# Where the split operands of the matmuls begin in SBUF: input at 128-byte lines, narrow products' weights 64 bytes on

## What is computed

```python
for i in range(DEPTH):                     # 4 layers
    kind, j = i % N_MIXERS, i // N_MIXERS  # mixers: MLA, MoBA, SSD, MLA
    h = rmsnorm(x, norm_mix[i])
    x = x + mixer(h)                       # MLA: 16 heads; MoBA: 8 heads; SSD: Mamba-2 scan, inner width 2048
    x = x + sq_relu_mlp(rmsnorm(x, norm_mlp[i]), mlp_w1[i], mlp_w2[i])
return rmsnorm(x, norm_final)

def sq_relu_mlp(h, w1, w2):
    a = jax.nn.relu(h @ w1)                # 1024 -> 4096
    return (a * a) @ w2                    # 4096 -> 1024
```

## Time and profile before

| | us |
|---|---|
| median of 3 runs | 1313.64 |
| lowest, highest | 1311.1, 1315.05 |
| span of the profiled execution | 1312.0 |
| TensorE matmul busy in it | 1286.5 (98%) |
| DVE busy | 891.4 (68%) |
| ACT busy | 671.6 (51%) |

### The profile page before, as it was taken

The page is one execution under the profiler, slowest core; times in us unless marked ns, Lnnn a source line. Parts: engine busy times, 40 slices in busy tenths (PEclk is TensorE's granted clock), DMA queues, the critical chain, the costliest instruction groups (busy, mean ns, idle before and its releaser), DMA issues.

```text
span 1312.0 us, 18369 instructions
## 1 busy us (share of the span) xinstructions
PE 1286.5 (98%) x7578; PEld 1126.3 (86%) x7578; DVE 891.4 (68%) x1180; ACT 671.6 (51%) x861; POOL 43.5 (3%) x58
## 2 busy tenths in 40 slices
PE   6999999999999999999999999999999999999998
PEld 5888888888999888887999888888887888888886
DVE  5877666665666666666899886766667876666664
ACT  5555554444555454444776644544445645454442
POOL 3000000000000000000101110000000000000000
PEclk9999999999999999999999999999999999999999
DMA  9744465555845475545574643755554334565540
GB/s 289 143 168 148 141 232 201 193 192 161 233 149 180 132 254 192 192 165 160 181 222 141 203 149 119 249 191 192 191 180 140 117 130 130 168 231 193 192 161 32
DMA packets 146067, 230.93 MB, mean 176 GB/s; under 512 B 7683, under 2 KB 112429, under 8 KB 145984
## 3 DMA queue, kind: packets, MB, share of 16 engines
q1 hardware_dynamic: 143136, 221.66, 50.8%
q0 software_dynamic: 2848, 8.10, 2.9%
HBM read 227.08 MB, written 2.65 MB: 175 GB/s over the span
## 4 chain that ended last, share of the span: by engine, by line
PE 88%; DVE 7%; DMA 1%; issue 1%; ACT 1%; POOL 1%; SPq 0%; POOLq 0%; DVEq 0%; ACTq 0%
PE bank L982 15%; PE acc L902 12%; PE acc L903 12%; PE acc L906 12%; PE bank L987 8%; PE bank L590 7%; PE bank L591 7%; PE bank L592 7%; DVE wlo L573 2%; PE bank L1402 1%; PE bank L1105 1%; PE bank L795 1%; PE bank L1408 1%; PE bank L1090 1%; DMA raw<-in_mla_w_in 1%
## 5 line engine op out<-in xcount | busy, mean ns | idle before, releaser
L573 DVE TENSOR_TENSOR wlo<-raw,whi 128x2048 fp32r<-128x2048 f32 (+2 forms) x207 | 464.7, 2255 | 139.6 <-ACT whi L557 139.5
L557 ACT ACTIVATE whi<-raw 128x2048 fp32r<-128x2048 f32 (+2 forms) x207 | 386.8, 1879 | 45.8 <-PE acc L906 44.2
L982 PE MATMUL bank<-hsplit,whi 128*128 128x512 f32 x896 | 212.2, 389 | 0.0
L903 PE MATMUL acc<-wlo,uhi 128*128 128x512 f32 x512 | 200.1, 391 | 0.0
L902 PE MATMUL acc<-whi,uhi 128*128 128x512 f32 x512 | 199.6, 390 | 0.0
L982 PEld LDWEIGHTS bank<-hsplit,whi 128*128 128x128 f32 x896 | 168.2, 188 | 34.9
L906 PE MATMUL acc<-whi,ulo 128*128 128x512 f32 x512 | 159.2, 390 | 0.0
L590 PE MATMUL bank<-hsplit,whi 128*128 128x256 f32 (+2 forms) x540 | 154.5, 286 | 0.3 <-DVE xn L1980 0.3
L592 PE MATMUL bank<-hsplit,wlo 128*128 128x256 f32 (+2 forms) x540 | 151.4, 280 | 0.0
L591 PE MATMUL bank<-hsplit,whi 128*128 128x256 f32 (+2 forms) x540 | 151.4, 280 | 0.0
L1027 ACT ACTIVATE relu<-bank 128x512 f32<-128x512 f32 x56 | 33.5, 598 | 188.9 <-PE bank L987 188.9
(11 more groups left out here) (252 smaller groups left out, 1813.4 us busy)
## 6 DMA issues: line engine op xcount, KB each, us to landing
raw<-in_mlp_w SPq DMA_DIRECT2D x128, 1024.0 KB, 5.5
raw<-in_ssd_w_in SPq DMA_DIRECT2D x18, 1024.0 KB, 5.4
raw<-in_mla_w_o SPq DMA_DIRECT2D x16, 1024.0 KB, 4.9
raw<-in_mla_w_ukv SPq DMA_DIRECT2D x8, 1024.0 KB, 5.8
raw<-in_moba_w_qkv SPq DMA_DIRECT2D x16, 512.0 KB, 5.3
raw<-in_ssd_w_out SPq DMA_DIRECT2D x8, 1024.0 KB, 4.9
raw<-in_mla_w_uq SPq DMA_DIRECT2D x8, 768.0 KB, 6.0
raw<-in_mla_w_in SPq DMA_DIRECT2D x4, 1024.0 KB, 7.5
```

Of the source, the lines that this page charges most:

```text
L557: nc.scalar.activation(whi[:, s, lo:e], raw[:, s, lo:e], ACT.Copy).then_inc(w_hi_done[s], 1)
L573: nc.vector.tensor_tensor(wlo[:, s, lo:e], raw[:, s, lo:e], whi[:, s, lo:e].bitcast(F32), ALU.subtract).then_inc(w_split[s], 1)
L903: nc.tensor.matmul(acc[t][half][:], lh, wl[:, k, n], start=False, stop=False)
L982: nc.tensor.matmul(ps, w[0][:, k, m * P:(m + 1) * P], hflat[:, k].rearrange("p a n -> p (a n)"), start=k == 0, stop=False)
```

## The change

`hsplit` becomes a plain array of 8 rows of 512 elements, used alike by all stages: input always at a line. The slots of `whi` and `wlo` become 32 elements longer (8320 bytes, 65 lines), and each unit's high and low part begin at an offset of 0 or 16 elements (64 bytes) in their slot, by kind: `ca`, `cb`, `down`, `wo`, `so` and `ukv` at 0 in both; `up` at 0 in `whi` and 16 in `wlo`; `kpe` with the first `uq`, the other `uq`, `mv`, `mqk`, `dt`, `cv` and `z` at 16 in both. ACT and DVE write, and `hi_lo` reads, at these offsets. The built program has the same instructions in the same order on all engines; `wlo` moves by 512 bytes, `x`, `xn`, `gbc` and `hsplit` by 1024, all else stays. As 65 is odd, slots 1 and 3 now begin at 0 modulo 256 and slots 0 and 2 at 128.

```diff
-        whi = sb("whi", [P, SLOTS, UNIT], F32R)
-        wlo = sb("wlo", [P, SLOTS, UNIT], F32R)
+        whi = sb("whi", [P, SLOTS, UNIT + 2 * HALF_LINE], F32R)
+        wlo = sb("wlo", [P, SLOTS, UNIT + 2 * HALF_LINE], F32R)
...
-        hrows = sb("hsplit", [P, KD, 2 * SEQ + 32], F32R)
-        hsplit = hrows[:, :, 16:16 + 2 * SEQ].rearrange("p k (a n) -> p k a n", a=2)
-        hflat = hrows[:].rearrange("p k n -> p (k n)")[:, 0:KD * 2 * SEQ].rearrange("p (k a n) -> p k a n", k=KD, a=2)
+        hsplit = sb("hsplit", [P, KD, 2, SEQ], F32R)
...
+        def start_of(kind):
+
+            if kind in ("ca", "cb", "down", "wo", "so", "ukv"):
+                return (0, 0)
+            return (0, HALF_LINE) if kind == "up" else (HALF_LINE, HALF_LINE)
...
         def hi_lo(key):
             off, a, b = view[key]
             s = first[key] % SLOTS
-            return (whi[:, s, off:off + a * b].rearrange("p (a b) -> p a b", a=a),
-                    wlo[:, s, off:off + a * b].rearrange("p (a b) -> p a b", a=a))
+            hi, lo = (off + start for start in starts[first[key]])
+            return (whi[:, s, hi:hi + a * b].rearrange("p (a b) -> p a b", a=a),
+                    wlo[:, s, lo:lo + a * b].rearrange("p (a b) -> p a b", a=a))
...
-                lo = 0
+                lo, high = 0, whi[:, s, starts[n][0]:starts[n][0] + e]
...
-                nc.scalar.activation(whi[:, s, lo:e], raw[:, s, lo:e], ACT.Copy).then_inc(w_hi_done[s], 1)
+                nc.scalar.activation(high[:, lo:e], raw[:, s, lo:e], ACT.Copy).then_inc(w_hi_done[s], 1)
...
-                nc.vector.tensor_tensor(wlo[:, s, lo:e], raw[:, s, lo:e], whi[:, s, lo:e].bitcast(F32),
+                nc.vector.tensor_tensor(low[:, lo:e], raw[:, s, lo:e], high[:, lo:e].bitcast(F32),
                                         ALU.subtract).then_inc(w_split[s], 1)
...
-        def split_input(j):
-
-            h = hflat if deferred(j) else hsplit
-            return h[:, :, 0, :], h[:, :, 1, :]
```

More of the change, by code:

```diff
@@ L34 @@
 UNIT = 2048
+HALF_LINE = 16
 AHEAD = 3
@@ L276, in build @@
         units, first = [], {}
+        starts = []
         view = {}
+        def start_of(kind):
+            if kind in ("ca", "cb", "down", "wo", "so", "ukv"):
+                return (0, 0)
+            return (0, HALF_LINE) if kind == "up" else (HALF_LINE, HALF_LINE)
         def unit(key, a, b, *srcs):
             first[key] = len(units)
+            starts.append(start_of(key if key == "dt" else key[0]))
             view[key] = (0, a, b)
@@ L288, in unit_of_two @@
             off, parts = 0, []
+            starts.append(start_of(keys[0][0]))
             for key, (a, b), src in zip(keys, shapes, srcs):
@@ L552, in act_splits @@
                     act.wait_ge(w_used[s], k)
-                lo = 0
+                lo, high = 0, whi[:, s, starts[n][0]:starts[n][0] + e]
                 if n in in_halves:
                     lo = e // 2
-                    nc.scalar.activation(whi[:, s, :lo], raw[:, s, :lo], ACT.Copy).then_inc(half_hi_done, 1)
-                nc.scalar.activation(whi[:, s, lo:e], raw[:, s, lo:e], ACT.Copy).then_inc(w_hi_done[s], 1)
+                    nc.scalar.activation(high[:, :lo], raw[:, s, :lo], ACT.Copy).then_inc(half_hi_done, 1)
+                nc.scalar.activation(high[:, lo:e], raw[:, s, lo:e], ACT.Copy).then_inc(w_hi_done[s], 1)
                 split_to["act"] += 1
@@ L565, in dve_splits @@
                 e = units[n][0] * units[n][1]
-                lo = 0
+                lo, high, low = 0, whi[:, s, starts[n][0]:starts[n][0] + e], wlo[:, s, starts[n][1]:starts[n][1] + e]
                 if n in in_halves:
@@ L569, in dve_splits @@
                     dve.wait_ge(half_hi_done, n + 1)
-                    nc.vector.tensor_tensor(wlo[:, s, :lo], raw[:, s, :lo], whi[:, s, :lo].bitcast(F32),
+                    nc.vector.tensor_tensor(low[:, :lo], raw[:, s, :lo], high[:, :lo].bitcast(F32),
                                             ALU.subtract).then_inc(half_split, 1)
                 dve.wait_ge(w_hi_done[s], k + 1)
-                nc.vector.tensor_tensor(wlo[:, s, lo:e], raw[:, s, lo:e], whi[:, s, lo:e].bitcast(F32),
+                nc.vector.tensor_tensor(low[:, lo:e], raw[:, s, lo:e], high[:, lo:e].bitcast(F32),
                                         ALU.subtract).then_inc(w_split[s], 1)
@@ L635, in act_scale_upper @@
                                  scale=rstd[:, j * T + t:j * T + t + 1]).then_inc(xn_upper_done, 1)
-        def split_input(j):
-            h = hflat if deferred(j) else hsplit
-            return h[:, :, 0, :], h[:, :, 1, :]
         def act_tr(act, j, t):
-            hhi, _ = split_input(j)
             for half in range(2):
@@ L719, in dve_tr @@
         def dve_tr(dve, j, t, halves=(0, 1)):
-            hhi, hlo = split_input(j)
             for half in halves:
@@ L981, in pe_up @@
                 for k in range(KD):
-                    nc.tensor.matmul(ps, w[0][:, k, m * P:(m + 1) * P], hflat[:, k].rearrange("p a n -> p (a n)"),
+                    nc.tensor.matmul(ps, w[0][:, k, m * P:(m + 1) * P], hsplit[:, k].rearrange("p a n -> p (a n)"),
                                      start=k == 0, stop=False)
@@ L986, in pe_up @@
                 for k in range(KD):
-                    mm = nc.tensor.matmul(ps[:, 0:SEQ], w[1][:, k, m * P:(m + 1) * P], hflat[:, k, 0, :], start=False,
+                    mm = nc.tensor.matmul(ps[:, 0:SEQ], w[1][:, k, m * P:(m + 1) * P], hsplit[:, k, 0, :], start=False,
                                           stop=k == KD - 1)
```

## The result

| | before | after |
|---|---|---|
| median, us | 1314.35 | 1321.75 |
| lowest, highest | 1311.1, 1315.71 | 1321.31, 1322.35 |
| span of the profiled execution | 1312.0 | 1319.7 |

The ratio is 1.0063, its 95% interval 1.0048 to 1.0078: the change makes the kernel 0.63% slower, about 7.4 us for the medians, 7.7 us for the spans. The prediction was 1303.0 us, range 1299.5 to 1310.5, so it missed the sign as well.

The account below looks back on a forecast made before the run. TensorE's summed matmul steps were taken to bound the kernel. The terms summed to -10.8 us, taken as -10.5: from the 1312.0 us span, plus 1.6 us around or between executions, to 1303 us, range 1299.5 to 1310.5.

Parts of the forecast that it names:

- item 10: ACT and DVE accessing most units 64 bytes past a line: 0, hidden under PE in any case.
- Item 9: Last L982 of each round, followed by a load of shifted low weights: 56 wide steps, 0 to +0.3 us, taken +0.15.
- Item 2: Narrow L987 products of the MLPs: 840 steps from 119.4 to 113.8 ns, -4.7 us.
- the first rival: Pair isn't symmetric: shifted stationary weights bring nothing in the mixers, half in items 2 to 4; 1310.5 us, chance 0.08.
- Item 1: Mixers' `mqk`, `cv`, `z`: 1248 narrow steps from 117.0 to 113.8 ns, -4.0 us.
- item 5: `kpe`: 48 steps from 117.0 to 113.8 ns, -0.15 us.
- Item 3: First two `up` units, low weights shifted: 128 of 384 steps from 120.0 to 113.8 ns, -0.8 us.
- Item 4: `uq` by head in MLA: 192 steps from 120.0 to 113.8 ns, -1.2 us; `ukv` 0.
- Item 6: MoBA's values, weights moving from 64 bytes past a line: 192 steps from 113.3 to 117.0 ns, +0.7 us.
- Item 7: Rotary part of `uq`, same pair as MoBA's values but from 120.0 ns: 96 steps, -0.3 us.
- Item 8: Wide `ca` and `cb`, input now at a line: 96 steps, -0.5 us if the input's place is the cause, else 0.
- two rivals: Odd slots slow some 1550 wide products: 5.5 ns each, 1311.5 us, chance 0.07; or 13.4 ns each, 1324 us, chance 0.04.

Follow-up runs that it names:

- slots_66_lines: The changed kernel with slots 66 lines apart, so all begin at 128 modulo 256, and `kp` moved: 1311.2 us, ratio 0.9978 to the kernel before.
- both_at_64: Changed kernel with slots of 66 lines, input at 192 modulo 256 everywhere, mixers' weights at 192, MLP weights at 128: 1315.08 us, ratio 1.0001 to the kernel before.
- input_64_everywhere: The kernel before with the input at 64 modulo 256 in every row of every stage, weights still at lines: 1314.15 us, ratio 0.9995.
- input_at_lines: The kernel before with the input at lines in all stages, slots of 64 lines and weights unshifted: 1319.5 us, ratio 1.0039.
- slots_65_lines: The kernel before with slots 65 lines apart instead of 64, no operand shifted by 64 bytes, `kp` moved: 1322.54 us, ratio 1.0064.
- input_192_everywhere: The kernel before with the input at 192 modulo 256 in every row of every stage, slots and weights unchanged: 1311.47 us, ratio 0.9974.

## Why the prediction was wrong, point by point

**The bound and its reading held.** TensorE's steps set the time: the sum of their changes is +8.1 us and the span changed by +7.7. Waits, ACT and DVE didn't matter (item 10, 0 forecast, DVE busy 891.2 for 891.4 us; the kinds with the two longer waits come to +0.7 us of the +8.1). Item 9, forecast +0.15, is 0: in slots_66_lines, with the same shifted loads, the wide steps are at 226.6 ns.

**First failed step: "the row that has this pair is that of MoBA's values ... 113.3 ns", taken as the step of the pair.** It was one of the pair's two levels. The same units at the same addresses took 117.8 ns in one kernel and 113.3 in another, and half of the mixers' pieces of the kernel before were at 117.8 and not at the 116.7 of the two stretches that were read. For the size that was forecast, every shifted narrow product would have had to be on the lower level.
- Item 2, L987, forecast -4.7: measured -1.5 (119.5 to 117.8 ns). After the wide products of a round, this pair always comes out on the upper level when the weights are the operand off the line, in all 56 rounds of after, and at 113.3 or 114.1 when the input is (both_at_64, input_64_everywhere). So the terms weren't symmetric in this place; the first rival had that idea but its ground was another.
- Item 1 (mixers) with item 5, forecast -4.15: measured -1.3, all of it in SSD (MoBA 0.0). 19 of 52 pieces got to 113.3 and 33 are at 117.8, where before 28 were at 116.7. That the kernel before already had a step of 116.7 in half of its pieces, by alternating 64 and 192, and that a piece on the upper level loses 1.1 ns against it, was not in the sum.
- Item 3, forecast -0.8: -0.5. Item 4, forecast -1.2: -0.4; in the first MLA stage and the second alike some heads are at 113.3, some at 117.8.
- Item 6, the "sharpest test", forecast +0.7: +0.4, with 117.6 ns in the stretch of the earlier trace rows. The value agreed and the inference from it was wrong: it was the other of two levels, in the same stage as queries and keys that didn't gain.
- Item 7, forecast -0.3: -0.2. Item 8, forecast -0.5: -0.1. Its idea was right and the odd slots hid it: with the input at a line and no odd slot the stretch of 232.4 ns is at 227.9 (input_at_lines), in after one of its two units lies in an odd slot and it is at 230.0.

**Second failed step: the odd slots, priced at nothing with 0.11 for two rivals.** The argument against them was that a wide step of 226.9 ns at 128/128 shows that nothing is taken from a moving stream. It shows that for this pair only, and no row had another. The rival named some 1550 wide products at 5.5 ns, +8.5 us. Measured: +10.7 us over 3103 products, 3.5 ns each in the mean. In the odd slots it is 5 to 6 ns (L983 of the first two MLPs from 226.7 to 232.9, output products of the last two from 227.9 to 232.7), and 2 to 3 ns in the even ones that follow (L983 of the last two MLPs 229.6, output products of the first two 229.7). The price was right; what was missed is the carry into the good slots, and the chance. Even with the narrow gains at 10.8 us that would have been no change (1314.35 - 10.8 + 10.7 = 1314.3); with the 3.5 us that came it is 1321.6, beside the measured 1321.75.

The rule of the Trainium skill weighed in the prediction, page "TensorE: Matmul & The Clock Gate", section "Step-by-step: what each phase is for", that two independent read ports keep weight loads and the running matmul out of each other's way, would have given no change at all. The runs don't agree with it for either kind of product: at a granted clock of nine tenths or more in all slices, the narrow step depends on the distance of its two operands (113.3, 117.8 or 120.0 ns), and the wide one too (226.7, 230.1, 233.3). Whether it is read bandwidth that they share, the runs don't show.

**What the runs support as the account.** Narrow products are slowest when the two operands begin at the same place modulo 256: 120.0 ns with both at 128 (input_at_lines) and with both at 192 (both_at_64). At 128 bytes apart the L987 of slots_65_lines take 119.1 ns. At a distance of 64 bytes they have two levels, 113.3 and 117.8, and stay on the one they reach after a pause.

For wide products the distance counts with its sign, and whether input or weights move changes the step by 1.2 ns at most. Taken is the start of the moving operand less that of the stationary one, modulo 256:

```text
distance     input moving (L982, L983)                 weights moving
0            226.7 ns (before)                         227.9 (ca, cb of input_at_lines)
64 bytes     230.1 (input_192_everywhere)              228.9 (ca, cb of input_64_everywhere)
128 bytes    232.9 (after, first two MLPs)             232.7 (after, outputs of the last two)
-64 bytes    233.3 (input_64_everywhere)               233.4 (ca, cb of input_192_everywhere)
```

(For `ca` and `cb` these are the 33 steps of the earlier trace rows, with the first few after the pause in them.) The 232.4 ns of the earlier trace rows, with the input at 64 and 192 by turns, lie between the two values for 64 bytes in the last column. For narrow products the sign doesn't tell the levels apart: the L988 of after are at 117.8 ns with the weights at 64 (odd slots) and 117.9 with them at 192 (even slots).

What inside the chip makes the distance count was not tried. What picks the level of a narrow stretch stays open too: the first steps differ from the pause on (226, 122, 122 against 222, 118, 122), but neither DVE's nor ACT's work was shown to cause it. Both operands of a wide product at one place other than 128 modulo 256 were not tried either.

## What to carry to other kernels

A layout's change moves every operand that shares the allocation: padding by one line shifted half of the slots by 128 bytes and cost more than the aimed shift brought. Pad by an even number of 128-byte lines (64 and 66 were measured here, against 65), and look at each place pair for wide and narrow products apart. A step read from one stretch may be one of two levels: read the same pair in several stretches before multiplying it by a thousand products, and give an address pair that no row shows a price and a real chance, in both directions.

## What had not been expected of the hardware

- One and the same narrow pair at 113.3 or at 117.8 ns for 187 steps on end, at a granted clock of 0.98 and 1.00 in the stretch from 620 to 700 us of the two kernels (the lower clock is with the shorter step).
- The penalty of a wide product outlasts its cause: nine products with good addresses after a series with bad ones are at 224 to 238 ns before 226.7 returns. Five at 228 to 236 ns come behind a series of narrow products even when all addresses are good.
- A wide product minds the sign of the distance: at 64 bytes one way it takes 230.1 or 228.9 ns, the other way 233.3 or 233.4.
- A shift of 32 or 96 bytes is no half of a shift of 64: 118.3 and mostly 118.8 ns in the mixers, against 113.3 or 117.8.
- Moving input off a line is worth more to a narrow product behind wide ones (113.3 at 192, 114.1 at 64 modulo 256) than weights off a line (117.8), with the same distance.
